# A hand-loaded activation set with logarithm and exponential in a two-block kernel

## The chip, the cores and the metric

The kernel runs on one core of one Trainium2 chip (trn2). The metric is the device time of one launch in microseconds. Five engines run side by side, each through its own list of instructions: TensorE (PE), VectorE (DVE), ScalarE (ACT), GpSimd (POOL) and SyncE (SP, which here only starts DMAs). They meet at semaphores. ScalarE evaluates its functions from tables; a set of functions is active at a time, and an instruction of its own, ACT_TABLE_LOAD, makes another set active.

## What is computed

Two transformer-like blocks, one after the other, on 512 tokens of width 1024, with 256 context tokens in the first, all in float32. Shortened from the reference:

```python
def rms(x, g):                                   # used ten times over tokens
    return x * rsqrt(mean(x * x, -1) + 1e-6) * g
# block 1
x = x + .5 * m[2] * swiglu(modulate(rms(x, g1), m[0], m[1]), w_in, w_out)      # and the same for the context
seg = modulate(rms(x, g2), m[3], m[4]) @ mix_w_in + b                          # context too
hm = mlstm(q, k, v, i, log_sigmoid(f))           # 8 heads, chunkwise, both directions
logf = log(lb + (1 - lb) * sigmoid(f)); k = (1 - lb) * sigmoid(-f)             # HGRN gates, 8 heads
o = (q * exp(b)) @ S + (q_t exp(b_t - b_s) k_s) v_s                            # b = cumsum(logf)
hh = head_rms(o) * silu(g)
x = x + m[5] * (sigmoid(gm) * (hm @ pm) + sigmoid(gh) * (hh @ ph)) @ w_out
x = rms(x + .5 * m[8] * swiglu(...), g_final)
# block 2
z = modulate(rms(x, n1), ...) @ w_in_2
attn = g0 * softmax(compressed) @ v + g1 * softmax(selected) @ v + g2 * softmax(window) @ v    # 8 heads of 64
ssm = glu(gelu(Re(C scan(a, B u)) + d * u))      # a = exp(lr*step) * (cos, sin)(li*step)
x = x + gt1 * concat(rms(attn), rms(ssm)) @ w_o
x = x + gt2 * (silu(a) * v) @ w_down             # (a, v) = causal conv(rms(x) @ w_up)
return rms(x, normf)
```

## The kernel before

The activations stay in SBUF, transposed: 128 rows of features by 512 tokens (256 for the context), eight such tiles for the width of 1024. Weights come in from HBM in tiles of 1 MB through four slots. In the feed-forwards each weight and activation is split into a rounded part and a rest (ScalarE writes `wh`, VectorE the rest `wl`), and TensorE runs three matmuls for one product; all matmuls are called through the helper at L300.

The stages follow one another: start (modulation rows, norms of x and context), feed-forward 1 (to about 680 us), the mixer's norms (to 714), the HGRN heads (to 1366), the mLSTM (to 1679), the merge (to 1988), feed-forward 2 (to 2381), the final norm of block 1 and the first of block 2, its projections (to 2564), the attention loop (to 2869), the gated output of the state-space branch, w2o (to 2952), feed-forward 3 and the last norm.

Nothing is scheduled by a planner. Each engine's order is written out by hand in a Python function per stage and engine (`act_...`, `dve_...`, `pool_...`, `pe_...`), and a wait stands where it is called: everything behind it on that engine waits too. For the HGRN heads and for the attention loop a list of items (`HG`, `B2`) is walked by all engines in the same order.

Where the change works:

- `act_stat` (L594 to L602) is ScalarE's part of a token norm: Square of each feature tile into two buffers, TensorE sums them through a matrix of ones (`pe_stat`, one matmul of two passes per tile, into a bank `ps`), then Ln (with scale 1/width and bias eps) and Exp with scale -0.5, which make the inverse root. It is called ten times; VectorE's and ScalarE's scaling waits for its Exp. In `act_ffn2` and `act_ffn3` the split of the first weight tile (L737) stands ahead of it.
- `act_hgrn` (L1135 to L1193): an item "fill" ends (at part 9) with Sigmoids of the gates and their Ln (L1160); "prep" is an Exp of a factor that GpSimd has subtracted (L1166); "state" holds further Exps; "out" is the head's output norm, Square (L1188), then Ln (L1191) and Exp (L1193). The item "out" of head h stands among the items of head h + 1, that of head 7 at the end.
- `act_mlstm` (L1401 to L1423): Exp and Ln(1 + .) of the forget gate (L1410, L1412), then Exps.
- `act_merge`: Ln and Exp of 32 columns of head norms (L1773, L1775).
- `act_att` (L2251 to L2330): in the loop over `B2`, item "exps" is the softmax's Exp of step n (L2278), "turned" the Copy of the transposed probabilities to SBUF (L2287, L2291) for TensorE's product with the values, "normed" the norm over 512 columns of a block of 128 tokens (Square L2299, Ln L2301, Exp L2303, Copy with scale L2305), "sin" the two Sin of a state-space step (L2328, L2330), in every second step. The compressed scores' Exp is L2261.

The kernel before names no set. When it is built, an ACT_TABLE_LOAD is put ahead of each activation whose function is not in the set that is active there: the first set in a fixed list that has the function. Ln and Exp get two different sets in this way. Such a load is put between the waits and the activation or ahead of them: an activation can carry a wait itself, and then the load ahead of it does not wait. In after.py the same placement still serves whatever the loads by hand leave open.

Of the kernel before, what the change touches and what calls it, by code (L numbers as in the profile page):

```python
# [317 lines left out]
def program(nc, dr, out_dram):  # L318
    ctx = ExitStack()
    with ctx:  # L320
        build(nc, dr, out_dram, ctx)


def build(nc, dr, out_dram, ctx):
# [33 lines left out]
    def rows(ap, k):  # L358
        return ap.rearrange("p (k t) -> p k t", k=k)
# [16 lines left out]
    def vec(n):  # L376
        o, c = VOFF[n]
        return VECS[:, o:o + c]
# [210 lines left out]
    def pool_start(e, w):  # L589
        ap, there = weight(("m8", 0, 1792))  # L590
        w.wait_ge(*there)
        e.tensor_copy(M8[:, :], ap).then_inc(*m8P.of("m8"))

    def act_stat(e, w, name, src, T, n_k, width, sq, rs, bank):  # L594
        for k in range(n_k):
            if k >= 2:
                w.wait_ge(*statP.at(name, k - 2))
            e.activation(sq[k % 2][:, 0:T], src[:, k, :], ACT.Square).then_inc(*statA.of(name, k))
        w.wait_ge(*statP.at(name, n_k - 1))
        e.activation(rs[:, 0:T], bank[:, 0:T], ACT.Ln, scale=1.0 / width, bias=eps).then_inc(*statA.of(name, "ln"))  # L600
        w.wait_ge(*statA.at(name, "ln"))
        e.activation(rs[:, 0:T], rs[:, 0:T], ACT.Exp, scale=-0.5).then_inc(*statA.of(name, "exp"))  # L602
# [527 lines left out]
    def act_hgrn(e, w):  # L1130
        for item, *a in HG:
            if item == "fill":
# [26 lines left out]
                for j in range(2):  # L1159
                    e.activation(z[f"b{j}"], z[f"b{j}"], ACT.Ln, scale=olb[:, j, h:h + 1],  # L1160
                                 bias=lb[:, j, h:h + 1]).then_inc(*fA.of(h, "ln", j))
            elif item == "prep":
                h, i = a
                r = RB[(14 * h + i) % 4]
                w.wait_ge(*rG.at(h, i, "k"))
                e.activation(r, r, ACT.Exp).then_inc(*rA.of(h, i))  # L1166
            elif item == "state":
                h, j, s = a
                d, b = DD[j], HD[h % 2][f"b{j}"]
                if s == 0:  # L1170
                    w.wait_ge(*sG.at(h, j, "c"))
                    e.activation(KS, KS, ACT.Exp).then_inc(*stA.of(h, j, "s"))
                    if h:
                        w.wait_ge(*oP.at(h - 1, "o"))
                    e.activation(d["qi"], b[:, 0:512], ACT.Exp).then_inc(*stA.of(h, j, "qi"))
                    e.activation(d["dc"], rows(b[:, 0:512], 4)[:, :, 127 if j == 0 else 0],
                                 ACT.Exp).then_inc(*stA.of(h, j, "dc"))
                elif s == 1:
                    w.wait_ge(*stP.at(h, j, "t1"))
                    e.activation(d["kn"][:, 0:512], banks("t1", h, j), ACT.Copy).then_inc(*stA.of(h, j, "k1"))  # L1180
                    w.wait_ge(*stP.at(h, j, "t2"))
                    e.activation(d["kn"][:, 512:768], banks("t2", h, j)[:, 0:256], ACT.Copy).then_inc(*stA.of(h, j, "k2"))
            elif item == "out":
                h, s = a
                if s == 0:
                    w.wait_ge(*oP.at(h, "o"))
                    w.wait_ge(*(fV.at(h + 1, "q") if h < 7 else oV.at(6, "u")))
                    e.activation(SB[0], banks("o", h), ACT.Square).then_inc(*oA.of(h, "sq"))  # L1188
                else:
                    w.wait_ge(*oP.at(h, "m"))  # L1190
                    e.activation(SB[0], banks("m", h), ACT.Ln, scale=1.0 / 128, bias=eps).then_inc(*oA.of(h, "ln"))  # L1191
                    w.wait_ge(*oA.at(h, "ln"))
                    e.activation(SB[0], SB[0], ACT.Exp, scale=-0.5).then_inc(*oA.of(h, "exp"))  # L1193
# [209 lines left out]
    def act_mlstm(e, w):  # L1403
        w.wait_ge(*endH[0].at(*endH[1:]))
        for k in range(1, KT, 2):
            src, dst = xp[:, k, :].rearrange("p (c r) -> p r c", r=8), xm[:, k, :].rearrange("p (r c) -> p r c", c=64)
            e.activation(dst, src, ACT.Copy).then_inc(*pmA.of("m", k))
        w.wait_ge(*pmV.at("m", KT - 2))
        w.wait_ge(*gtV.at("abs"))
        e.activation(LFs, LFs, ACT.Exp).then_inc(*gtA.of("exp"))  # L1410
        w.wait_ge(*gtA.at("exp"))
        e.activation(LFs, LFs, ACT.Ln, bias=1.0).then_inc(*gtA.of("ln"))  # L1412
        for j in range(2):
            R = slice(32 * j, 32 * j + 32)
            w.wait_ge(*gtV.at("neg", j))
            e.activation(gr[R, 512:768], gr[R, 512:768], ACT.Exp, bias=nmc[R]).then_inc(*gtA.of("wc", j))
            w.wait_ge(*gtV.at("M", j))
            e.activation(wi[R, :], Mr[R, :], ACT.Exp, scale=-1.0, bias=mC[R]).then_inc(*gtA.of("wi", j))
            w.wait_ge(*gtV.at("gu", j))
            e.activation(gu[R, :], gu[R, :], ACT.Exp, scale=-1.0).then_inc(*gtA.of("gu", j))  # L1420
        for i in range(4):
            w.wait_ge(*mlP.at("k", i))
            e.activation(kt[:, i, :], banks("k", i), ACT.Identity, bias=vec("mb_k")[:, i:i + 1]).then_inc(*mlA.of("k", i))  # L1423
# [828 lines left out]
    def act_att(e, w):  # L2252
        w.wait_ge(*cpV.at("vc"))
        w.wait_ge(*cgV.at("all"))
        w.wait_ge(*c2L.at("c2"))
        for item, n, *more in B2:
            if item == "comp":
                s = more[0]
# [52 lines left out]
            elif item == "tables":  # L2311
                i = n
                c, s = SC2[i % 2]
                if i >= 2:
                    w.wait_ge(*s5V.at(i - 2, "im"))
                    w.wait_ge(*s5G.at(i - 2, "im"))
                e.activation(s, iot, ACT.Copy, scale=c16["ph"][:, i:i + 1]).then_inc(*s5A.of(i, "sn"))
                e.activation(c, iot, ACT.Identity, scale=c16["ph"][:, i:i + 1], bias=quarter).then_inc(*s5A.of(i, "cs"))
                b = banks("bt", i)
                w.wait_ge(*s5P.at(i, "t"))  # L2320
                if i >= 2:
                    w.wait_ge(*s5P.at(i - 2, "I"))
                e.activation(BT[i % 2][0], b[:, 0:128], ACT.Copy).then_inc(*s5A.of(i, "q1"))
                e.activation(BT[i % 2][1], b[:, 128:256], ACT.Copy).then_inc(*s5A.of(i, "q2"))
            elif item == "sin":
                c, s = SC2[n % 2]
                w.wait_ge(*s5G.at(n, "cs"))
                e.activation(c, c, ACT.Sin, scale=TWO_PI).then_inc(*s5A.of(n, "cos"))  # L2328
                w.wait_ge(*s5V.at(n, "sn"))
                e.activation(s, s, ACT.Sin, scale=TWO_PI).then_inc(*s5A.of(n, "sin"))  # L2330

    def pool_att(e, w):
        for item, n, *more in B2:
# [462 lines left out]
```

## Time and profile before

| | us |
|---|---|
| three timed runs | 3377.4, 3379.3, 3381.4 (median 3379.3) |
| the profiled execution, its own time | 3383.4 |
| its span, first to last instruction | 3381.4 |
| TensorE busy in it | 3057.6 (90%) |
| VectorE | 1485.7 (44%) |
| ScalarE | 1036.6 (31%) |
| GpSimd | 527.7 (16%) |
| mean granted TensorE clock | 0.932 of 2.4 GHz |

A row of a timeline reads: start, duration, engine, line, operation, written tile <- read tiles, shapes, count; in brackets the idle time of that engine ahead of it and what ended it. Rows that follow one another closely are merged, with their count and whole duration. A helper's line (L300) stands for all its callers, so the tiles tell which call it is. A row of the waits reads: who waited for whom, microseconds in total, times, the longest. The windows give, for each stretch, the busy time and count of each engine, then PEclk, the granted TensorE clock (1.00 is 2.4 GHz, 0.50 is 1.2 GHz, between them a mixture), then the share of the DMA engines and GB/s. The busy shares are averages over stages that have different bounds; what ScalarE's time is worth shows only where another engine waits for it.

### The profile page before, as it was taken

To read this page: it belongs to the slowest core of one execution; us is meant where nothing else is said; L and a number is where in the kernel's file an instruction comes from. 1 tells how busy PE (TensorE), PEld (TensorE's weight loads), DVE (VectorE), ACT (ScalarE), POOL (GpSimd) and SP (SyncE) were. 2 spreads that over 40 slices of the span, in tenths; PEclk is the share of its full clock that TensorE was granted. 3 is DMA by queue.
4 is the path that set the end of the run, shared out by engine and by line. 5 is a ranking of instruction groups with operands and counts; after the bars stand their busy time and mean duration, and the time that the engine had idled before them with its cause. 6 is when DMAs were issued, how large, how long until landed. Compare 5 with 4: busy or idle time off the path is not lost.

```text
span 3381.4 us, 32985 instructions
## 1 busy us (share of the span) xinstructions
PE 3057.6 (90%) x13464; PEld 2269.8 (67%) x13464; DVE 1485.7 (44%) x2473; ACT 1036.6 (31%) x1605; POOL 527.7 (16%) x498
## 2 busy tenths in 40 slices
PE   7999999979888987898899989999798788999997
PEld 3888888846666665665566567877356555377785
DVE  0866555215444556305731142332214887143443
ACT  3311111143333344103421132222313556152432
POOL 0000010004322233000001101000002655010210
PEclk9999999989999998998899999999995787999999
DMA  7344444021101000210021222222121000222220
GB/s 276 122 165 181 152 160 153 15 81 38 38 26 38 25 13 1 91 62 13 13 75 75 83 86 93 95 97 83 38 75 50 7 7 13 88 86 87 81 95 36
DMA packets 36726, 254.82 MB, mean 75 GB/s; under 512 B 4064, under 2 KB 4192, under 8 KB 10080
## 3 DMA queue, kind: packets, MB, share of 16 engines
q1 hardware_dynamic: 36576, 252.73, 20.6%
q8 instruction: 106, 1.74, 0.2%
q14 instruction: 44, 0.36, 0.0%
HBM read 250.61 MB, written 2.10 MB: 75 GB/s over the span
## 4 chain that ended last, share of the span: by engine, by line
PE 79%; DVE 10%; ACT 6%; POOL 2%; issue 2%; DMA 0%; DVEq 0%; SPq 0%; POOLq 0%; another core or an unknown queue 0%; ACTq 0%
PE ps L300 78%; DVE xm L1238 1%; DVE at L1245 1%; POOL tb L2351 1%; DVE xs L767 1%; DVE t L762 0%; DVE wb L2486 0%; DVE hd L1212 0%; POOL kb L2339 0%; DVE hd L1214 0%; ACT hd L1152 0%; ACT L602 0%; ACT hd L1150 0%; ACT L600 0%; POOL cs L2341 0%
## 5 line engine op out<-in xcount | busy, mean ns | idle before, releaser
L300 PE MATMUL ps<-xs,wh 128*128 128x512 f32 (+1 forms) x3328 | 955.2, 372 | 30.5 <-DVE xs L767 20.6
L300 PEld LDWEIGHTS ps<-xs,wh 128*128 128x128 f32 x3328 | 603.8, 190 | 147.7 <-issue 24.4
L300 PE MATMUL ps<-xs,wl 128*128 128x512 f32 (+1 forms) x1664 | 614.5, 369 | 0.0
L300 PE MATMUL ps<-h,wh 128*128 128x512 f32 (+1 forms) x1408 | 402.9, 373 | 34.9 <-POOL h L906 34.9
L743 DVE TENSOR_TENSOR wl<-w,wh 128x2048 fp32r<-128x2048 f32 (+3 forms) x122 | 264.6, 2168 | 229.0 <-ACT wh L737 229.0
L737 ACT ACTIVATE wh<-w 128x2048 fp32r<-128x2048 f32 (+3 forms) x122 | 221.0, 1811 | 440.0 <-PE ps L300 361.2
L300 PEld LDWEIGHTS ps<-xs,wl 128*128 128x128 f32 x1664 | 316.3, 190 | 53.6
L300 PEld LDWEIGHTS ps<-h,wh 128*128 128x128 f32 x1408 | 260.0, 194 | 81.9 <-issue 37.6
L300 PE MATMUL ps<-h,wl 128*128 128x512 f32 (+1 forms) x704 | 261.3, 371 | 0.0
L300 PE MATMUL ps<-xp,w 128*128 128x512 f32 x512 | 231.4, 597 | 10.7 <-ACT xp L1005 10.7
L906 POOL TENSOR_TENSOR h<-t,h 128x512 fp32r<-128x512 f32 x66 | 73.0, 1111 | 944.3 <-ACT h L839 944.3
L300 PE MATMUL ps<-xm,w 128*128 128x512 f32 (+1 forms) x464 | 176.1, 549 | 21.7 <-DMA w<-in_wgate 11.2
L698 DVE SCALAR_TENSOR_TENSOR sq<-w,small,sq 128x256 f32<-128x256 f32 x392 | 180.8, 483 | 10.0
L300 PEld LDWEIGHTS ps<-xm 128*128 128x128 f32 x896 | 124.1, 205 | 79.8 <-issue 74.7
L300 PE MATMUL ps<-xm 128*128 128x128 f32 x896 | 127.2, 290 | 49.2 <-DVE xm L1238 49.2
L300 PEld LDWEIGHTS ps<-xp,w 128*128 128x128 f32 x512 | 94.1, 192 | 109.4 <-issue 98.2
L300 PEld LDWEIGHTS ps<-xm,w 128*128 128x128 f32 x464 | 90.8, 227 | 104.6 <-issue 102.9
L884 DVE SCALAR_TENSOR_TENSOR x<-ps,small,x 128x512 f32<-128x512 f32 x80 | 60.0, 750 | 220.8 <-PE ps L300 220.8
L300 PEld LDWEIGHTS ps<-h,wl 128*128 128x128 f32 x704 | 136.6, 194 | 22.6
L839 ACT ACTIVATE h<-t 128x512 fp32r<-128x512 f32 x66 | 37.0, 560 | 372.1 <-DVE t L862 372.1
L1113 POOL TENSOR_TENSOR xm<-hd 128x256 f32<-128x256 f32 x112 | 84.9, 758 | 382.0 <-DVE hd L1212 294.4
L862 DVE TENSOR_TENSOR t<-t,ps 128x512 f32<-128x512 f32 x66 | 39.5, 599 | 197.3 <-PE ps L300 191.5
(388 smaller groups left out, 4133.3 us busy)
## 6 DMA issues: line engine op xcount, KB each, us to landing
w<-in_ada SPq DMA_DIRECT2D x60, 1024.0 KB, 4.8
w<-in_f1i SPq DMA_DIRECT2D x22, 1024.0 KB, 5.7
w<-in_f2i SPq DMA_DIRECT2D x22, 1024.0 KB, 4.8
w<-in_f3i SPq DMA_DIRECT2D x22, 1024.0 KB, 4.8
w<-in_whf SPq DMA_DIRECT2D x8, 1024.0 KB, 4.8
w<-in_whqg SPq DMA_DIRECT2D x8, 1024.0 KB, 4.7
w<-in_wgg SPq DMA_DIRECT2D x8, 1024.0 KB, 6.8
w<-in_wpp SPq DMA_DIRECT2D x8, 1024.0 KB, 4.8
```

The lines of the kernel that those rows point to most:

```text
L300: return e.matmul(out, l, r, start=st, stop=sp)
L698: e.scalar_tensor_tensor(out=a, in0=wv[:, k, :], scalar=v[:, k:k + 1], in1=a, op0=ALU.mult, op1=ALU.add).then_inc(*mvV.of(n, c, k))
L737: e.activation(hi[:, 0:key[2]], ap, ACT.Copy).then_inc(*hiA.of(key))
L743: e.tensor_tensor(lo[:, 0:key[2]], ap, hi[:, 0:key[2]].bitcast(F32), ALU.subtract).then_inc(*loV.of(key))
L767: e.scalar_tensor_tensor(out=lo[:, k, :], in0=ybuf[(i - 1) % 3][:, 0:T], scalar=shift[:, k:k + 1], in1=hi[:, k, :].bitcast(F32), op0=ALU.a ...
L839: e.activation(hh_[:, q, o:o + T], s[:, 0:T], ACT.Copy).then_inc(*hidA.of(F.name, j, x))
L862: e.tensor_tensor(s, s, banks(F.name, j, 1, x)[:, 0:T], ALU.mult).then_inc(*gateV.of(F.name, j, x))
L884: e.scalar_tensor_tensor(out=dst[:, m, :], in0=banks(F.name, n, "dn", m, x)[:, 0:T], scalar=g[:, m:m + 1], in1=dst[:, m, :], op0=ALU.mult, ...
L906: e.tensor_tensor(hl_[:, q, o:o + T], s, hh_[:, q, o:o + T].bitcast(F32), ALU.subtract).then_inc(*hidP.of(F.name, j, x))
L1113: e.tensor_tensor(rv[:, :, qh, :], b4[:, :, qh, :], mid, ALU.subtract).then_inc(*rG.of(h, i, "q"))
L1238: e.tensor_tensor(Ev[:, :, kh, :], rv[:, :, kh, :], factor_views(z[f"k{j}"][:, 0:512], hf)[:, :, kh, :], ALU.mult).then_inc(*eV.of(h, i, "k"))
L1245: e.copy_predicated(rows(AT[j][h % 2], 4), m8v[:, j, n, :].unsqueeze(1).to_broadcast([128, 4, 128]), rows(banks("prod", h, i), 4)).then_in ...
```

## The change

A function `logs` loads the set `natural_log_exp_and_others`, which holds Ln and Exp. It is called at the start of every `act_stat`, after the two gate Ln of each HGRN head, after the Ln of the mLSTM gates (ahead of which the set `natural_log` is loaded by hand), at the start of the attention loop behind its three waits, and after the second Sin of each state-space step. While that set is active no further load is placed for Ln, Exp, Square, Copy or Identity.

```diff
--- before.py
+++ after.py
@@ -591,7 +591,12 @@
         w.wait_ge(*there)
         e.tensor_copy(M8[:, :], ap).then_inc(*m8P.of("m8"))
 
+    def logs(e):
+
+        e.preload_act_table_set("natural_log_exp_and_others")
+
     def act_stat(e, w, name, src, T, n_k, width, sq, rs, bank):
+        logs(e)
         for k in range(n_k):
             if k >= 2:
                 w.wait_ge(*statP.at(name, k - 2))
@@ -1159,6 +1164,7 @@
                 for j in range(2):
                     e.activation(z[f"b{j}"], z[f"b{j}"], ACT.Ln, scale=olb[:, j, h:h + 1],
                                  bias=lb[:, j, h:h + 1]).then_inc(*fA.of(h, "ln", j))
+                logs(e)
             elif item == "prep":
                 h, i = a
                 r = RB[(14 * h + i) % 4]
@@ -1408,8 +1414,10 @@
         w.wait_ge(*pmV.at("m", KT - 2))
         w.wait_ge(*gtV.at("abs"))
         e.activation(LFs, LFs, ACT.Exp).then_inc(*gtA.of("exp"))
+        e.preload_act_table_set("natural_log")
         w.wait_ge(*gtA.at("exp"))
         e.activation(LFs, LFs, ACT.Ln, bias=1.0).then_inc(*gtA.of("ln"))
+        logs(e)
         for j in range(2):
             R = slice(32 * j, 32 * j + 32)
             w.wait_ge(*gtV.at("neg", j))
@@ -2253,6 +2261,7 @@
         w.wait_ge(*cpV.at("vc"))
         w.wait_ge(*cgV.at("all"))
         w.wait_ge(*c2L.at("c2"))
+        logs(e)
         for item, n, *more in B2:
             if item == "comp":
                 s = more[0]
@@ -2328,6 +2337,7 @@
                 e.activation(c, c, ACT.Sin, scale=TWO_PI).then_inc(*s5A.of(n, "cos"))
                 w.wait_ge(*s5V.at(n, "sn"))
                 e.activation(s, s, ACT.Sin, scale=TWO_PI).then_inc(*s5A.of(n, "sin"))
+                logs(e)
 
     def pool_att(e, w):
         for item, n, *more in B2:
```

The program has 114 table loads before and 79 after: 36 by hand through `logs`, one by hand of `natural_log`, 42 placed by the build. All else stays in its order.

ScalarE at the mixer's norm of x (`act_stat` "mx", then `act_shift`), before:

```order
L598 ACTIVATE t<-x 128x512 [waits ffn_acc]
L598 ACTIVATE t<-x 128x512
L598 ACTIVATE t<-x 128x512 [waits stat_pe] x6
L600 ACT_TABLE_LOAD
L600 ACTIVATE t<-ps,small 128x512 [waits stat_pe]
L602 ACT_TABLE_LOAD
L602 ACTIVATE t<-t 128x512 [waits stat_act]
```

and in the change:

```order
L596 ACT_TABLE_LOAD [waits ffn_acc]
L603 ACTIVATE t<-x 128x512 x2
L603 ACTIVATE t<-x 128x512 [waits stat_pe] x6
L605 ACTIVATE t<-ps,small 128x512 [waits stat_pe]
L607 ACTIVATE t<-t 128x512 [waits stat_act]
```

One load instead of two, and it carries the wait for the feed-forward (`ffn_acc`) that the first Square carried.

ScalarE around the output norm of HGRN head 5, in the items of head 6 (`hd`, `xm` gates and factors, `s` the norm's buffer), before:

```order
L1160 ACT_TABLE_LOAD
L1160 ACTIVATE hd<-hd,small 128x768 [waits hg_fill_act]
L1160 ACTIVATE hd<-hd,small 128x768
L1166 ACT_TABLE_LOAD
L1166 ACTIVATE xm<-xm 128x512 [waits hg_log_pool] x4
L1188 ACTIVATE s<-ps 128x512 [waits hg_fill_dve,hg_out_pe]
L1166 ACTIVATE xm<-xm 128x512 [waits hg_log_pool]
L1191 ACT_TABLE_LOAD
L1191 ACTIVATE s<-ps,small 128x512 [waits hg_out_pe]
L1193 ACT_TABLE_LOAD
L1193 ACTIVATE s<-s 128x512 [waits hg_out_act]
```

and in the change:

```order
L1165 ACT_TABLE_LOAD
L1165 ACTIVATE hd<-hd,small 128x768 [waits hg_fill_act]
L1165 ACTIVATE hd<-hd,small 128x768
L596 ACT_TABLE_LOAD
L1172 ACTIVATE xm<-xm 128x512 [waits hg_log_pool] x4
L1194 ACTIVATE s<-ps 128x512 [waits hg_fill_dve,hg_out_pe]
L1172 ACTIVATE xm<-xm 128x512 [waits hg_log_pool]
L1197 ACTIVATE s<-ps,small 128x512 [waits hg_out_pe]
L1199 ACTIVATE s<-s 128x512 [waits hg_out_act]
```

The load behind the gate Ln stands where it stood, with another set; the two of the output norm are gone.

ScalarE in the attention loop, at the first Sin (`cs` its tables, `pt` the transposed probabilities), before:

```order
L2328 ACT_TABLE_LOAD
L2328 ACTIVATE cs<-cs 128x512 [waits s5_pool]
L2330 ACTIVATE cs<-cs 128x512 [waits s5_dve]
L2287 ACTIVATE pt<-ps 128x256 [waits att_turn_pe]
L2278 ACT_TABLE_LOAD
L2278 ACTIVATE xm,small<-ps,small 128x128 [waits att_max]
```

and in the change:

```order
L2337 ACT_TABLE_LOAD
L2337 ACTIVATE cs<-cs 128x512 [waits s5_pool]
L2339 ACTIVATE cs<-cs 128x512 [waits s5_dve]
L596 ACT_TABLE_LOAD
L2296 ACTIVATE pt<-ps 128x256 [waits att_turn_pe]
L2287 ACTIVATE xm,small<-ps,small 128x128 [waits att_max]
```

The load for Exp has moved ahead of the Copy.

## Rows read from the trace of the kernel before

**Rows 1.** The page: busy time by engine; the chain that ended last, by engine.

```profile
PE 3057.6 (90%) x13464; PEld 2269.8 (67%) x13464; DVE 1485.7 (44%) x2473; ACT 1036.6 (31%) x1605; POOL 527.7 (16%) x498
...
PE 79%; DVE 10%; ACT 6%; POOL 2%; issue 2%; DMA 0%; DVEq 0%; SPq 0%; POOLq 0%; another core or an unknown queue 0%; ACTq 0%
```

**Rows 2.** Timeline, the mixer's norm of x.

```profile
680.00 7.49 PE L300 MATMUL ps<-t,cst 128*128 128x512 f32 x16 [1.33 <-ACT t L598]
...
686.33 1.28 ACT L600 ACT_TABLE_LOAD   x1
687.63 0.69 ACT L600 ACTIVATE t<-ps,small 128x512 f32<-128x512 f32 x1
688.33 1.28 ACT L602 ACT_TABLE_LOAD   x1
```

**Rows 3.** Windows: sums of the norm at 2383 and of that at 2891.

```profile
2383.00:2386.00 3.00, 3.00 (x7) 1.18 (x8) 0.00 (x0) 1.66 (x4) 0.00 (x0) 1.00 0.00 0
...
2891.30:2894.00 2.70, 2.63 (x4) 1.23 (x5) 0.00 (x0) 1.17 (x3) 0.00 (x0) 0.61 0.72 303
```

**Rows 4.** Timeline, TensorE's sums in three norms, with the idle time ahead.

```profile
1990.71 9.18 PE L300 MATMUL ps<-t,cst 128*128 128x512 f32 x16 [3.40 <-ACT t L598]
...
2382.94 7.49 PE L300 MATMUL ps<-t,cst 128*128 128x512 f32 x16 [1.60 <-ACT t L598]
...
2891.37 5.40 PE L300 MATMUL ps<-tb,cst 128*128 128x512 f32 x8 [2.17 <-ACT tb L598]
```

**Rows 5.** Timeline, start: first Squares, and TensorE's modulation rows.

```profile
11.44 1.15 ACT L598 ACTIVATE sq<-x 128x512 f32<-128x512 f32 x2 [4.67 <-DMA x<-in_x]
...
32.18 41.60 PE L300 MATMUL ps<-w,small 128*2 128x256 f32 x192
```

**Rows 6.** Timeline, the mixer's norm of the context: sums and Ln.

```profile
696.98 6.15 PE L300 MATMUL ps<-t,cst 128*128 128x256 f32 x16 [9.49 <-ACT t L598]
...
703.69 0.47 ACT L600 ACTIVATE t<-ps,small 128x256 f32<-128x256 f32 x1
```

**Rows 7.** Waits of TensorE in the HGRN stage, 790 to 1372 us.

```profile
PE ps L1346 <- DVE xc L1260: 5.6, 1, 5.6
```

**Rows 8.** Timeline, output norms of heads 6 and 7: mean, then Ln.

```profile
1324.57 1.08 PE L300 MATMUL ps<-s,cst 128*128 128x512 f32 x2
...
1326.30 0.69 ACT L1191 ACTIVATE s<-ps,small 128x512 f32<-128x512 f32 x1
...
1360.20 1.13 PE L300 MATMUL ps<-s,cst 128*128 128x512 f32 x2 [0.69 <-ACT s L1188]
...
1361.46 0.69 ACT L1191 ACTIVATE s<-ps,small 128x512 f32<-128x512 f32 x1
```

**Rows 9.** Timeline, the merge's head norms: VectorE's reductions and Ln.

```profile
1688.40 4.68 DVE L1812 TENSOR_REDUCE small<-xmc 128x8 f32<-128x1024 f32 x4
...
1693.14 0.32 ACT L1773 ACTIVATE small<-small 128x32 f32<-128x32 f32 x1
```

**Rows 10.** Timeline, ScalarE's entry into the attention loop.

```profile
2571.83 1.28 ACT L2261 ACT_TABLE_LOAD   x1 [7.54 <-DVE xm L2380]
```

**Rows 11.** Timeline, a Copy behind Sin and the product that reads it.

```profile
2589.21 0.36 ACT L2287 ACTIVATE pt<-ps 128x256 f32<-128x256 f32 x1
...
2592.48 0.66 PE L300 MATMUL ps<-vn,pt 128*128 128x64 f32 x4
```

**Rows 12.** Waits of TensorE in the attention loop, 2570 to 2905 us.

```profile
PE ps L2581 <- DVE bb L2454: 37.6, 11, 7.7
PE ps L2574 <- ACT rp L2305: 14.9, 3, 10.8
```

**Rows 13.** Timeline, the end of the attention loop: TensorE and GpSimd.

```profile
2867.88 1.12 PE L2574 MATMUL ps<-cst,rp 128*128 128x128 f32 x4 [10.84 <-ACT rp L2305]
2868.79 4.92 PE L300 MATMUL ps<-wb,w 128*128 128x512 f32 x8
...
2868.96 1.65 POOL L2358 TENSOR_TENSOR wb<-wb,tb 128x512 f32<-128x512 f32 x1 [1.23 <-DVE wb L2488]
```

## The prediction

> **What bounds the kernel now.** I read the profile in this order: busy time by engine, the chain that ended last, then, for every place that the change touches, the timeline of all engines around it, the waits of TensorE and the granted clock. Busy time and chain say that TensorE is the bound: 90% of the span busy, 79% of the chain, while ScalarE is busy 31% and holds 6% of the chain [rows 1]. So a table load taken from ScalarE is worth something only where TensorE (or, in the attention loop, VectorE) is waiting for the ScalarE instruction behind it. By the order of instructions the program has 114 table loads before and 79 after. 35 loads of 1.28 us are 44.9 us of ScalarE; the question is how much of that lies on the path.
>
> **A norm.** Of a norm (the eight Squares, Ln, Exp) the reader is to see two things [rows 2]. The load ahead of Ln starts at 686.33, right behind the last Square, while TensorE still sums that Square until 687.49 (680.00 + 7.49); Ln starts at 687.63. So this load is covered but for 0.14 us. The load ahead of Exp (688.33) has no cover: Ln has just ended. The change removes both and puts one load ahead of the first Square. There ScalarE has just been released by a wait, and a load put in by hand stands behind that wait, where one put in by the builder stands ahead of it (the order rows show which instruction carries the wait). Nothing covers it, because the Squares, and TensorE's sums of them, are what everybody waits for. One load with its gap is 1.30 us. A norm is then: + 1.30 (new) - 1.30 (Exp's) - 0.14 (Ln's open rest) = -0.1.
>
> **The clock in a norm.** What precedes the sums decides how long they take. Where TensorE has been idle 1.60 us, the 16 matmuls take 7.49 us and the granted clock stays 1.00 (2.4 GHz); after 2.17 us idle it is 0.61 over the first stretch, that is mostly the 1.2 GHz level, and after 3.40 us idle the 16 matmuls take 9.18 us [rows 3, 4]. Three norms start warm today: the one at 680 (idle 1.33, [rows 2]), the one at 2383 (idle 1.60) and the last one of the kernel (7.49 us as well). The new load lengthens these idles to 2.6, 2.9 and 2.9 us, beyond the 2.17 us after which the clock is seen to fall. I take the fall in all three: 3 x (9.18 - 7.49) = +5.1. Its bounds are 0 and 5.1. The other norms start cold anyway.
>
> **All norms.** The first pair, on x and on the context, is special. The Squares on x start when their DMA has landed, and the load now stands behind that wait. The context's Squares follow with a second load of a set that is already active. TensorE's 192 matmuls for the modulation rows follow without a gap until 73.8 [rows 5], so what is late at their start is late at their end; the values of Ln and Exp are wanted only after them. From the start: + 1.3 - 0.1 - 1.3 + 1.3 = +1.2. The norm of the context after the first feed-forward sums half as many columns, so its Ln load is covered less: the sums end at 703.13, Ln starts at 703.69 [rows 6]; + 1.3 - 1.3 - 0.5 = -0.5. Six more norms (at 680, 1990, 2383, 2399, 2955, 3362) give -0.1 each, -0.7 with rounding. The norm of the four tiles behind the gate of the state-space branch gives 0. Together 0.0. Loading a set that is already active was not seen; I take the full 1.28 us, for a load is a copy whatever was there, and keep 0 as its other end for four of these loads.
>
> **HGRN heads.** Per head the change removes the two loads of the output norm (Ln, Exp), and moves the load of the first factor's Exp to stand right behind the two gate Ln, where its neighbours in ScalarE's order are the same: the move is worth nothing. In heads 0 to 5 the output norm falls in a stretch in which TensorE works through the next head's projections: in the whole stage TensorE waits once for the factor chain behind an output norm (L1346, 5.6 us) [rows 7], and that is at head 6, with no projections left. There TensorE has the mean ready at 1325.65 and Ln starts at 1326.30; without loads Ln starts 0.6 earlier and Exp a further 1.3. At head 7 it is 1361.33 against 1361.46, so 0.1 + 1.3 [rows 8]. Behind it hang the output, the slot for the gate weights and their DMA, all of which move along. HGRN: -1.9 - 1.4 = -3.3.
>
> **mLSTM and merge.** In the mLSTM gates a load stays before Ln and one moves; TensorE is busy all through, 0. In the merge, Ln starts at 1693.14 because VectorE reduces until 1693.08 (1688.40 + 4.68): its load was covered. Exp's load was not, and TensorE waits for what hangs on it [rows 9]: -1.3.
>
> **Attention loop.** Its first load waits with ScalarE for VectorE and sits open on the chain (2571.83) [rows 10]; by hand it is placed ahead of that wait: -1.3. In the 16 steps with Sin, the load for Exp moves ahead of the Copy between them. Exp comes when it did. The Copy comes 1.28 us later, and TensorE's value product reads it; here the Copy ends at 2589.57 and the product starts at 2592.48 [rows 11], the smallest gap I found in these steps, so it stays covered: 0. The four norms of 512 columns lose two loads each. TensorE waits three times for them, 14.9 us in all and 10.8 the longest, so 4.1 in the other two; but in the same loop it waits 37.6 us for VectorE's tables [rows 12], which shows VectorE to be the next bound there. Bounds 0 and -4.1; I take -0.4, near the VectorE end. The last of the four ends the loop: TensorE starts at 2867.88 for it and would start 2.6 earlier. But the last state sums need GpSimd's xi, done at 2870.61 (2868.96 + 1.65). Today TensorE's eight matmuls run from 2868.79 to 2873.71 [rows 13], the first four at about 0.85 us each; begun at 2866.2, four end at 2869.6, the other four wait until 2870.65 and end at about 2872.4: -1.3, with 0 and -2.6 as bounds.
>
> **The sum.** Norms 0.0, HGRN -3.3, merge -1.3, entry of the loop -1.3, its norms -0.4, its end -1.3: -7.6. With the clock of three norms, +5.1: -2.5. The profiled execution took 3383.4 us, its span 3381.4, and the median of the runs is 3379.3; I apply the difference to the median: 3376.8. All of this is near 0.1%, and 0.2% (6.8 us) is about what a measurement of this kernel can tell from no change.
>
> A rule of the skill speaks for more. The Trainium skill, "ScalarE: Activation LUTs", section "Rules for kernel authors", says that a kernel needing Exp and Ln should use the set that holds both, for one load and not two. The trace agrees on the price of a load but not on its worth: in a norm the first of the two is under TensorE's sums and the new one is open. The same page, "What ACT_TABLE_LOAD costs", adds a drain to each switch, 2.66 us in all; the trace has Ln start 0.02 us behind its load's end. With 2.66 for 1.30, -7.6 would be some -14 and the time about 3370.
>
> **Rivals.** (1) The clock stays at 2.4 GHz in all three norms, their idles being still under the 3.40 us that surely lost it: -7.6, 3371.7. For it: only one row lies between 1.60 and 3.40. Chance 0.17. (2) Every load counts, as a rule that counts loads would have it: 35 x 1.28, 3334.4. Against it speaks the whole of [rows 1]. Chance 0.02. (3) Loading an active set is nearly free: four loads less (context, context after the feed-forward, and the norms at 2399 and 2955): -2.5 - 5.1 = -7.6, also 3371.7. Chance 0.05. (4) Slower: the Copies are on the path after all. It decides where less than 1.28 us lies between a Copy and the product that reads it; if all 16 steps give up 1.28, + 20.5 - 2.5 = +18.0, 3397.3; five of them suffice to be slower than before. The gap of 2.9 us speaks against it. Chance 0.05. (5) The removed waits only let TensorE run into VectorE or a DMA sooner, so that HGRN and merge give back half, with the falls: -0.2, 3379.1. Chance 0.11. My forecast: 0.60.
>
> **Numbers.** 3376.8 is the forecast; a fall in one or two norms only gives 3375.1 or 3373.4, inside it. The range 3370.5 to 3381.5 takes in (1), (3) and (5), the full 4.1 of the attention norms on one side and none of the uncertain gains on the other, and leaves out (2), (4) and the tails. Faster by over 0.2% needs (1), (3) or (2), in part, 0.2; slower is (4) and a tail, 0.06; within 0.2% 0.74.
>
> **What would show it.** ScalarE's busy time falls by about 45 us and the span by 3. In a norm, a load of 1.28 us ahead of the Squares with nothing beside it, and Ln and Exp without. A granted clock near 0.5 in the sums at 681, 2384 and 3364, their 16 matmuls at over 9 us. The rows product at start beginning 1.2 later; TensorE's wait at L1346 (now L1352) shorter by 1.9 and its wait ahead of the merge by 1.3. If the three norms keep 7.49 us, the clock step is wrong; if Copies show TensorE waiting in the loop, (4) is right.

## The result: 0.2% slower in one comparison, even in the second, and the profile after

Thirteen executions each, in one comparison: 3386.3 us (median, 3379.6 to 3390.7) against 3378.6 for the kernel before; ratio 1.0021, interval 1.0013 to 1.0030. A second comparison of the same two kernels, below, gave 1.0001 (0.9990 to 1.0012). Over all 27 executions of the changed kernel and all 75 of the kernel before on record, the means are 3384.4 and 3380.8: +3.5 us, 0.10%. These come from several comparisons, whose medians for the kernel before alone lie between 3378.6 and 3382.5, so the pooled figure is rough. The prediction, 3376.8 with a range up to 3381.5, is wrong: the gain that it forecast came in neither comparison, and the first one lies outside the range.

The page of the changed kernel, to be held against [rows 1]: span, busy time by engine, the chain by engine.

```profile
span 3387.5 us, 32949 instructions
...
PE 3070.5 (91%) x13464; PEld 2278.5 (67%) x13464; DVE 1487.9 (44%) x2473; ACT 994.3 (29%) x1570; POOL 528.1 (16%) x498
...
PE 79%; DVE 11%; ACT 5%; POOL 2%; issue 2%; DMA 0%; DVEq 0%; SPq 0%; POOLq 0%; another core or an unknown queue 0%; ACTq 0%
```

ScalarE lost 42.3 us of work, near the 44.9 us of 35 loads. TensorE became 12.9 us *busier* with the same 13,464 matmuls. In these traces matmuls of one shape take longer where the granted clock is lower ([rows 3, 4]: sums at 1.00 and at 0.61), and the mean clock fell from 0.932 to 0.929: the first hint.

The mixer's norm, timeline; it answers to [rows 2]:

```profile
679.08 1.28 ACT L596 ACT_TABLE_LOAD   x1 [20.11 <-DVE xc L889]
680.38 1.15 ACT L603 ACTIVATE t<-x 128x512 f32<-128x512 f32 x2
681.15 7.49 PE L300 MATMUL ps<-t,cst 128*128 128x512 f32 x16 [2.61 <-ACT t L603]
...
688.68 0.69 ACT L605 ACTIVATE t<-ps,small 128x512 f32<-128x512 f32 x1 [1.22 <-PE ps L300]
689.40 0.63 ACT L607 ACTIVATE t<-t 128x512 f32<-128x512 f32 x1
```

The load stands open ahead of the Squares; Ln and Exp follow without one. From the start of the sums to the start of Exp it is 8.25 us, before 9.62: 1.37 less, for 1.28 more of idle time ahead of the sums. The norm gives back what the load took, and 0.1. The sums keep 7.49 us although TensorE was idle for 2.61 ahead of them. All 36 loads of the joint set take the same time, also the four that find it active:

```profile
L596 ACT ACT_TABLE_LOAD  x36: 1283/1283/1283, 11.7 to 3365.2; - x36
```

Two more norms, at 1993 and at the end of the kernel; and the eight sums behind the gate of the state-space branch. The first and the third answer to [rows 4]:

```profile
1992.67 9.81 PE L300 MATMUL ps<-t,cst 128*128 128x512 f32 x16 [4.82 <-ACT t L603]
...
3367.26 10.30 PE L300 MATMUL ps<-t,cst 128*128 128x512 f32 x16 [2.88 <-ACT t L603]
...
2896.91 3.83 PE L300 MATMUL ps<-tb,cst 128*128 128x512 f32 x8 [3.45 <-ACT tb L603]
```

The last norm in the kernel before:

```profile
3362.61 7.49 PE L300 MATMUL ps<-t,cst 128*128 128x512 f32 x16 [1.60 <-ACT t L598]
```

The last norm lost the clock after 2.88 us idle (0.70 over its 16 sums); the one at 2385, after the same 2.88, did not (7.49). And behind the gate TensorE was idle 3.45 us, longer than the 2.17 of [rows 4], and its sums took 3.83, at clock 1.00, in place of 5.40. How long it was idle does not decide this alone.

**Where the time went.** Every kernel here has the same 13,464 matmuls in the same order, so the start of the n-th one can be compared between two traces. The columns give how much later the changed kernel leaves each stage than it entered it, for two pairs: the first two traces (spans 3387.5 and 3381.4), and two further executions of the same kernels described below (3378.2 and 3375.9). The figures in brackets are the falls of the clock that the prediction put on three norms.

| stage | predicted | first pair | second pair |
|---|---|---|---|
| start, to the modulation rows | +1.2 | -0.1 | +0.7 |
| feed-forward 1 | 0 | 0.0 | +1.6 |
| norms at 680 and 697 | -0.6 (+1.7) | +0.1 | +0.2 |
| HGRN heads, to the gate weights | -3.3 | -2.1 | -3.3 |
| mLSTM | 0 | +1.6 | -0.3 |
| merge | -1.3 | -0.3 | -0.7 |
| its projections, to 1990 | 0 | +1.4 | 0.0 |
| norm at 1990 | -0.1 | +0.7 | +1.3 |
| feed-forward 2 | 0 | -0.3 | -0.1 |
| norms at 2383 and 2399, first projections | -0.2 (+1.7) | +1.7 | +2.0 |
| further projections | 0 | +1.7 | +1.6 |
| entry of the attention loop | -1.3 | -1.4 | -1.4 |
| the loop, its norms, its end | -1.7 | +1.3 | +1.5 |
| gated output, w2o | 0 | -0.7 | -0.7 |
| norm at 2955, feed-forward 3 | -0.1 | -0.2 | -0.1 |
| last norm, to the end | -0.1 (+1.7) | +2.7 | 0.0 |
| sum | -2.5, with +5.1 for the clock | +6.1 | +2.3 |

In the first pair eight stages lose time, and two of them (3.1 us) contain nothing that the change touches; in the second pair it is two of seven (3.2 us). The +1.6 of the mLSTM, where one load has moved and one is another set's, is not in the second pair.

One of these losses is no scatter. From the first matmul behind the norm at 2399 to the last projection ahead of the attention loop, the same 462 matmuls, first in the kernel before and then in the changed one (window, its length, busy time and count of each engine, granted clock, DMA share, GB/s):

```profile
2413.50:2564.40 150.90, 139.09 (x462) 84.14 (x462) 32.69 (x86) 21.93 (x49) 8.88 (x7) 0.90 0.17 64
```

```profile
2414.90:2568.70 153.80, 141.99 (x462) 86.26 (x463) 32.68 (x86) 21.91 (x49) 8.87 (x7) 0.88 0.18 63
```

The 2.9 us are TensorE's busy time: 1.3 of them arise within 6 us of the first of these matmuls, 1.6 from 2530 to 2537, behind a pause of 3.2 us that is the same in both kernels. Both traces of the kernel before take 150.9, all four of the changed kernel 153.8 to 153.9, and the kernels of experiments 1, 2 (the norms' loads alone) and 5 below 153.7 to 153.9; the three that leave the norms as they were take 150.9 to 151.1, and those of experiments 4 and 7 149.2. So this loss goes with where the loads of the norms stand, in every trace. How they cause it is not shown: the kernel of experiment 1 pays it too, though TensorE idles no longer ahead of its sums than before.

### The profile page after: what moved, and what is told of

Its sections match the earlier page's. It is cut to its first block, busy times and chain, and to the rows that moved or that the text cites. A ratio compares the mean times of both kernels' runs of the same rounds, so it can differ in the third digit from the quotient of the medians.

```text
span 3387.5 us, 32949 instructions
## 1 busy us (share of the span) xinstructions
PE 3070.5 (91%) x13464; PEld 2278.5 (67%) x13464; DVE 1487.9 (44%) x2473; ACT 994.3 (29%) x1570; POOL 528.1 (16%) x498
## 4 chain that ended last, share of the span: by engine, by line
PE 79%; DVE 11%; ACT 5%; POOL 2%; issue 2%; DMA 0%; DVEq 0%; SPq 0%; POOLq 0%; another core or an unknown queue 0%; ACTq 0%
PE ps L300 79%; DVE xm L1244 1%; POOL tb L2361 1%; DVE at L1251 1%; DVE wb L2496 1%; DVE xs L772 1%; DVE t L767 0%; POOL kb L2349 0%; DVE hd L1218 0%; ACT L596 0%; DVE wb L2492 0%; DVE hd L1220 0%; ACT hd L1157 0%; POOL cs L2351 0%; ACT hd L1155 0%
```

## Experiments

**1. The load behind the Squares.** The same load and count, placed later:

```diff
     def act_stat(e, w, name, src, T, n_k, width, sq, rs, bank):
-        logs(e)
         for k in range(n_k):
...
+        logs(e)
         w.wait_ge(*statP.at(name, n_k - 1))
```

> The changed kernel with one thing moved: in each of the eleven norms the load of the joint set stands behind the last Square, ahead of the wait for TensorE's sums, and no longer ahead of the first Square. 79 loads as in the changed kernel. Theory A (the load ahead of the Squares is open, 1.30 us in each norm, and lengthens the idle time of TensorE that precedes the sums, so that the clock falls in some): the last norm's 16 sums are back at 7.49 us (10.30 in the changed kernel), each norm ends about 1.3 earlier than in the changed kernel, and the whole is 10 to 16 us faster than the changed kernel, that is 3 to 9 us faster than the kernel before (ratio 0.9974 to 0.9991). Theory B (the norms are nearly even, and the attention loop and its Copies make the kernel slower): 0 to 4 us faster than the changed kernel, ratio 1.001 to 1.002. Theory C (the joint set itself makes its instructions slower): as the changed kernel, 1.002.

Measured: 3369.9 us, ratio 0.9966 (0.9954 to 0.9978), 12.6 below the median of the kernel before. Against the changed kernel in the same comparison it is 12 below the mean and 9.7 below the median, where theory A gave 10 to 16. (There are ten norms; "eleven" was a miscount.) Theory A holds in size for the step between the two kernels; the gain over the kernel before is more than the 3 to 9 us that it gave, since the changed kernel was no slower than that one here. B and C fall. The last norm's sums are back at 7.50 us. The norm at 1990 in this kernel:

```profile
1979.39 9.06 PE L300 MATMUL ps<-t,cst 128*128 128x512 f32 x16 [3.40 <-ACT t L602]
...
1986.64 0.63 ACT L602 ACTIVATE t<-x 128x512 f32<-128x512 f32 x1 [0.23 <-PE ps L300]
1987.29 1.28 ACT L596 ACT_TABLE_LOAD   x1
1988.59 0.69 ACT L605 ACTIVATE t<-ps,small 128x512 f32<-128x512 f32 x1
1989.31 0.63 ACT L607 ACTIVATE t<-t 128x512 f32<-128x512 f32 x1
```

The load lies where the load ahead of Ln lay in [rows 2], beside TensorE's last sum, and serves Exp as well.

**2. The norms alone, and all but the norms.** The first adds to the kernel before only

```diff
     def act_stat(e, w, name, src, T, n_k, width, sq, rs, bank):
+        logs(e)
```

and the second takes only this line from the changed kernel.

> The kernel before with the new load ahead of the first Square of each norm, and nothing else of the change: 104 loads. Theory A (the norms hold the loss): slower than before by 6 to 10 us, ratio 1.0018 to 1.0030. Theory B (the attention loop holds it): ratio 0.9995 to 1.0005. By the stages of the two traces so far, the norms at 1990, 2383 and 3362 us end 0.7, 1.2 and 2.7 us later.

> The changed kernel without the load in the norms (they keep the loads ahead of Ln and of Exp as before); HGRN heads, merge and attention loop as changed: 89 loads. Theory A: 1 to 5 us faster than the kernel before, ratio 0.9985 to 0.9997. Theory B: 4 to 7 us slower, ratio 1.0012 to 1.0021.

Measured, norms alone: 3391.2 us (3380.6 to 3397.0), ratio 1.0022 (1.0010 to 1.0034). All but the norms: 3380.6, ratio 0.9996 (0.9988 to 1.0005). So what loses lies in the norms, and what the rest brings is not the 7.6 us predicted for it, but 1.9, within what the comparison can tell from nothing.

**3. The changed kernel again, three times, and the kernel before again.** No edit.

> The changed kernel once more, for the scatter between profiled executions: which differences of a stage come again. Every theory: ratio 1.0013 to 1.0030. Theory A: the sums of the last norm take 9 us or more again, and the norms at 680 and 2383 keep 7.49. If the differences inside the attention loop and of the granted clock ahead of it (2536 us) come with another sign, they are scatter and no effect of the change.

> The changed kernel, one more execution, to compare one of its shorter executions (3377 to 3381) with its longer ones (3387 to 3392) stage by stage. Theory G: they differ only where the granted clock differs: in the norms (the last one 7.49 against 10.30), in the feed-forwards and in the attention loop, with waits for other engines alike. Rival: one stage holds the 10 us, with a wait of its own.

> As the look before it: the changed kernel, one more execution. Theory G: sums of the norms at 680 and 2383 can take 7.49 or over 9 us from one execution to the next. Rival: they are the same in each.

> The kernel before, one more execution. Theory G: its stages differ from those of its first trace only by the granted clock, up to 2 us in mLSTM (where three kernels lost 1.4 us and four did not) and up to 4 us in the attention loop; its norms at 680, 2383 and 3362 take 7.49 us again, since they follow after 1.33 and 1.60 us without work.

Measured: the repeat gave ratio 1.0001, outside what every theory had said, with eight executions from 3376.7 to 3380.0 and four from 3388.8 to 3392.3. Two single executions gave 3391.8 and 3380.3, so one of each sort has a trace; the kernel before gave 3377.8. The page's busy time, first of the longer and then of the shorter one:

```profile
span 3389.8 us, 32949 instructions
...
PE 3071.2 (91%) x13464; PEld 2280.4 (67%) x13464; DVE 1487.0 (44%) x2473; ACT 994.1 (29%) x1570; POOL 528.1 (16%) x498
```

```profile
span 3378.2 us, 32949 instructions
...
PE 3060.1 (91%) x13464; PEld 2271.2 (67%) x13464; DVE 1486.1 (44%) x2473; ACT 993.6 (29%) x1570; POOL 528.4 (16%) x498
```

11.1 of the 11.6 us are TensorE's busy time. No stage holds them: by the start of the same matmuls the longer one loses 2.6 at the start, 1.6 in feed-forward 1, 1.5 in HGRN, 1.8 in mLSTM, 1.5 at 1938, 2.9 in feed-forward 2, and nothing from there to the end, the attention loop among it. At 1938 nothing stands but a matrix product; a window there in the longer and then in the shorter one (busy time and count of each engine, granted clock, DMA share, GB/s):

```profile
1938.00:1948.00 10.00, 7.78 (x19) 4.26 (x19) 6.04 (x9) 2.43 (x2) 1.66 (x1) 0.83 0.50 195
```

```profile
1929.00:1939.00 10.00, 7.78 (x24) 4.03 (x23) 5.10 (x7) 2.44 (x2) 1.66 (x1) 1.00 0.42 153
```

TensorE is busy 7.78 of 10 us in both; in one the clock dips, in the other it doesn't, and then 24 matmuls run in the time of 19. Theory G holds in that the clock makes the difference. Its places are wrong: the attention loop differs by nothing, and the sums at 680 and 2383 took 7.49 us in all four traces of the changed kernel, those of the last norm in three of the four. The kernel before shows the same: its second trace is 5.5 us shorter than its first, 4.9 of it TensorE's busy time (3052.7 for 3057.6), with 1.7 at the start and 3.1 in feed-forward 1 and nothing in the mLSTM or the attention loop, where up to 2 and up to 4 had been expected; its three warm norms took 7.49 again. The Trainium skill, "TensorE: Matmul & The Clock Gate", Part 1, says that the same kernel meets the clock gate differently from one run to the next. The traces agree, with 11.1 us of TensorE's busy time between two executions of this kernel.

Of the 27 executions of the changed kernel 11 took over 3387 us, of the 75 of the kernel before 3; of the 12 with the norms' loads alone 7 did; of the 33 of the three kernels that leave the norms as they were (all but the norms, and experiment 6), none took over 3384.4. Within the second comparison alone it is 4 of 12, 3 of 30, 7 of 12 and 0 of 11.

**4. Early: the load ahead of the wait.** At the six places where the norm finds another set, for instance

```diff
         act_ffn(e, w, F2)
+        logs(e)
         w.wait_ge(*end2[0].at(*end2[1:]))
         act_stat(e, w, "fin", xv, TL, KT, D, f2_tmp, f2_tmp[2], banks("fin"))
```

and none in the four others, which find it active: 75 loads, four fewer than in experiment 1.

> The changed kernel with the norm's load written ahead of the wait that precedes the norm (so that it falls into idle time of ScalarE), and left out in the four norms that find the joint set already active: 75 loads. Theory A (a norm costs what is open in it, and a load behind a wait is open): TensorE's idle time ahead of the sums is back at 1.33 and 1.60 us (2.6 and 2.9 in the changed kernel), Ln and Exp have no load ahead; each norm is as short as in the kernel with the late load or 0.1 to 0.6 shorter, the time 3366 to 3371, ratio 0.9955 to 0.9978. Rival D (the late load gained by something else than the load's place, such as a draw of the clock): 3375 or more, ratio 0.998 or more.

Measured: 3367.1 us, ratio 0.9956 (0.9944 to 0.9969). It is the best kernel of the study, 14.2 us below the median of the kernel before in its comparison. The last norm:

```profile
3330.68 1.28 ACT L596 ACT_TABLE_LOAD   x1
3348.78 1.15 ACT L602 ACTIVATE t<-x 128x512 f32<-128x512 f32 x2 [16.81 <-DVE x L889]
```

```profile
3349.55 7.49 PE L300 MATMUL ps<-t,cst 128*128 128x512 f32 x16 [1.60 <-ACT t L602]
...
3357.08 0.69 ACT L604 ACTIVATE t<-ps,small 128x512 f32<-128x512 f32 x1 [1.22 <-PE ps L300]
3357.80 0.63 ACT L606 ACTIVATE t<-t 128x512 f32<-128x512 f32 x1
```

The load takes 1.28 us of 18 in which ScalarE has nothing to do, and TensorE's idle time is back at 1.60. Rival D falls: two kernels with different places of the load, both covered, agree within 3 us.

**5. Double: two loads ahead of the Squares.**

```diff
     def act_stat(e, w, name, src, T, n_k, width, sq, rs, bank):
+        e.preload_act_table_set("natural_log")
         logs(e)
```

> The changed kernel with two loads ahead of the Squares of each norm (first the set of the logarithm, then the joint one): 89 loads. Theory A: each of the ten norms ends 1.30 us later than in the changed kernel, 10 to 13 us in all, and where TensorE is then idle for more than 4 us ahead of the sums, these take 9 us or more in all norms, also at 680, 2383 and 3362: 12 to 20 us slower than the changed kernel, ratio to the kernel before 1.0035 to 1.0065. Rival (the loads are covered and only the draw of the clock differs): ratio 1.000 to 1.0025.

Measured: 3403.2 us, ratio 1.0063 (1.0050 to 1.0076), at the upper end of theory A, 19 us above the mean of all executions of the changed kernel. The last norm, which answers to the two above:

```profile
3375.91 1.28 ACT L599 ACT_TABLE_LOAD   x1 [18.10 <-DVE x L890]
3377.20 1.28 ACT L596 ACT_TABLE_LOAD   x1
...
3379.27 9.06 PE L300 MATMUL ps<-t,cst 128*128 128x512 f32 x16 [4.17 <-ACT t L604]
```

Now all three warm norms lose the clock: 9.88 us after 3.90 idle at 685, 9.06 after 4.17 at 2393 and here. So up to 2.88 us of idle time the clock nearly always held in these three places, and at 3.90 and 4.17 us it did not. Elsewhere the same does not hold, as the gate branch shows. In one table, the time from TensorE's last matmul ahead of a norm to its first behind it (the last norm has none behind; its 16 sums stand there):

| norm | before | changed | norms alone | late | early | double |
|---|---|---|---|---|---|---|
| 680 and 697 | 35.2 | 35.3 | 35.3 | 32.7 | 32.4 | 40.0 |
| 1990 | 17.8 | 18.5 | 18.7 | 16.4 | 16.3 | 19.7 |
| 2383 and 2399 | 32.2 | 32.6 | 32.7 | 30.1 | 29.8 | 36.6 |
| gate branch | 7.4 | 7.1 | 10.0 | 5.8 | 8.0 | 10.5 |
| 2955 | 17.7 | 17.7 | 18.3 | 14.9 | 17.4 | 20.2 |
| last, sums | 7.5 | 10.3 | 7.5 | 7.5 | 7.5 | 9.1 |

One profiled execution each, so a unit or two is the clock's; but the first three rows show the order plainly. Covered, the joint set is worth 1.0 to 1.5 us for each norm of the first three rows (two of them hold two norms); open, nothing or less.

**6. The parts outside the norms, one at a time.** To the kernel before are added, in the first kernel, the loads in HGRN and mLSTM (the merge follows from the set that is then active); in the second, those of the attention loop:

```diff
                                  bias=lb[:, j, h:h + 1]).then_inc(*fA.of(h, "ln", j))
+                logs(e)
...
+        e.preload_act_table_set("natural_log")
         w.wait_ge(*gtA.at("exp"))
         e.activation(LFs, LFs, ACT.Ln, bias=1.0).then_inc(*gtA.of("ln"))
+        logs(e)
```

```diff
         w.wait_ge(*c2L.at("c2"))
+        logs(e)
         for item, n, *more in B2:
...
                 e.activation(s, s, ACT.Sin, scale=TWO_PI).then_inc(*s5A.of(n, "sin"))
+                logs(e)
```

> The kernel before with the change in the HGRN heads, the mLSTM gates and the merge alone. The prediction gave -3.3 and -1.3: 4.6 us faster, ratio 0.9986. By the stages of the traces of the changed kernel, -2.1 in the heads, 0 to +1.4 in mLSTM, -0.3 in the merge: 0.6 to 2.4 faster, ratio 0.9990 to 1.0000.

> The kernel before with the change in the attention loop alone. The prediction gave -3.0 us, ratio 0.9991. By the stages of the traces of the changed kernel the entry gives -1.4 and the rest of the loop takes 1 to 3 back: ratio 0.9998 to 1.0005. If the Copies of the Sin steps were on the path, over 1.002.

Measured: HGRN to merge 3378.2 us, ratio 0.9992 (0.9983 to 1.0001); attention 3381.7, ratio 1.0002 (0.9993 to 1.0011). The interval of the first holds both its values. The second is on the side of the stages: no gain where 3 us were predicted. TensorE's waits in the loop of the second say where they went, against [rows 12] (2568 to 2903 us, the same columns):

```profile
PE ps L2587 <- DVE bb L2460: 46.4, 11, 7.7
PE ps L2580 <- ACT rp L2310: 7.8, 1, 7.8
```

The wait for the loop's norms fell by 7.1 us, the wait for VectorE's tables rose by 8.8. The wait for the Copy that a Sin load delays stays at 0.8 us, once, as before. That VectorE took the gain back is read from these waits and not isolated, for the loop's length also moves with the clock: without any edit in it, it took 306.4 us in both traces of the kernel before, 302.2 with the norms' loads alone and 302.8 in the first kernel here, with TensorE busy 248.4, 239.2 and 246.0 (the same 939 matmuls, behind the entry).

**7. The loop as before, behind the early norms.** From kernel 4 the load behind the two Sin is taken out:

```diff
                 e.activation(s, s, ACT.Sin, scale=TWO_PI).then_inc(*s5A.of(n, "sin"))
-                logs(e)
```

> The kernel with the early norm loads, without the load behind each pair of Sin: in the attention loop only the load at the entry is written by hand, the rest is placed as in the kernel before (82 loads). Theory E (the joint set in the loop gains nothing, since TensorE's wait for the loop's norms goes over to VectorE, and the two executions with and without it differ by -2 to +4 us through the clock): within 3 us of the kernel with the early loads, 3364 to 3368, ratio 0.9950 to 0.9965; TensorE waits some 15 us for the loop's norms and some 37 us for VectorE's tables, in place of 8 and 46. Theory F (the loads behind Sin delay the loop by 2 us or more): 3362 to 3365, ratio 0.9940 to 0.9952. By the prediction's terms, which gave the norms and the end of the loop 1.7 us: 3368 to 3370.

Measured: 3368.2 us, ratio 0.9965 (0.9952 to 0.9979), at the upper edge of theory E and at the lower one of the prediction's terms; one microsecond can't be told here. The waits are 12.9 for the norms and 43.3 for the tables, not the 15 and 37 expected: together 56.2 with the old loop and 54.6 (7.8 and 46.8) with the new one. The loop's loads are worth nothing that these runs can measure.

## Why the prediction failed, step by step

Two steps failed. The clock term was put on three norms (+5.1) and at nothing everywhere else: the norms' clock held in eleven of twelve cases, and the clock was lost in stages that the prediction had at 0. And the attention loop's norms and end, at -1.7, measured +1.3 and +1.5. The steps in order:

**The norm's arithmetic** held at 680 (-0.1, measured -0.1, idle time and sums to Exp together). It failed at 1990: there TensorE has been idle 4.82 us in place of 3.40 and more of its sums run at 1.2 GHz, 9.81 us for 9.18. A norm that starts cold can get worse too; I had taken it to be without risk. In all four traces of the changed kernel these sums took 9.78 to 10.41. At the start the rows product begins 1.4 us later on the mean of five traces with the change (32.15) than of five with the old start (30.72); predicted +1.2, near it, though the first pair alone (32.04 and 32.18) hides it and the two groups overlap (31.18 to 33.75, and 30.13 to 32.18).

**The clock step** had the right sign and the wrong place; that its size, 5.1, is of the order of what the clock took elsewhere is chance. I took one row (2.17 us idle, clock 0.61) as the point at which the clock falls, and put +1.7 on each of three norms. In twelve such norms (three in each of four traces) it fell once, and in the three of the kernel with the norms' loads alone not at all. The loss came elsewhere, in stages that the sum has at 0: 2.9 us in the projections ahead of the attention loop in every trace of the changed kernel, and in the longer executions also in feed-forward 1, the mLSTM, the products to 1990 or feed-forward 2. With the norms' loads alone the kernel is 8.7 us slower by the medians, where the table of norms and the start account for about 6, 2.6 of it at the gate branch; the rest is not placed. Its one trace is of a shorter execution (3385.4), in which the projections take 2.9 more than before and the loop 4.2 less. I had written that a trace can be compared with a trace and the difference put on the median; with executions that spread over 15.6 us (3376.7 to 3392.3 in the second comparison), and where 11.1 of the 11.6 us between two traced ones are TensorE's busy time, that holds for no effect of 3 us.

**HGRN** was right. TensorE's longest wait at L1352 is 3.7 us, 5.6 in [rows 7] (a second, short one there makes 5.0 in all); head 7 is shorter by 1.4. The waits of the changed kernel, then head 7 before and changed:

```profile
PE ps L1352 <- DVE xc L1266: 5.0, 2, 3.7
```

```profile
1364.12 0.75 DVE L1279 SCALAR_TENSOR_TENSOR s<-ps,vec,s 128x512 f32<-128x512 f32 x1 [8.57 <-ACT s L1193]
```

```profile
1360.58 0.69 ACT L1197 ACTIVATE s<-ps,small 128x512 f32<-128x512 f32 x1 [1.22 <-PE ps L300]
1361.30 0.63 ACT L1199 ACTIVATE s<-s 128x512 f32<-128x512 f32 x1
1361.96 0.75 DVE L1285 SCALAR_TENSOR_TENSOR s<-ps,vec,s 128x512 f32<-128x512 f32 x1 [7.19 <-ACT s L1199]
```

It answers to [rows 8]; VectorE's idle time fell from 8.57 to 7.19 us. The stage is 3.3 us shorter in the second pair, 2.1 in the first, whose clock dipped before head 7.

**The merge** was right where it was argued. VectorE waits 0.65 us for Exp, 1.96 before, 1.3 less. Before, then changed:

```profile
1695.03 4.63 DVE L1818 TENSOR_TENSOR hn<-hn,small 128x1024 f32<-128x1024 f32 x4 [1.96 <-ACT small L1775]
```

```profile
1692.71 0.32 ACT L1781 ACTIVATE small<-small 128x32 f32<-128x32 f32 x1 [1.29 <-DVE small L1820]
1693.06 0.23 ACT L1783 ACTIVATE small<-small 128x32 f32<-128x32 f32 x1
...
1693.32 4.63 DVE L1826 TENSOR_TENSOR hn<-hn,small 128x1024 f32<-128x1024 f32 x4 [0.65 <-ACT small L1783]
```

Of this the stage keeps 0.3 in the first pair and 0.7 in the second.

**The entry of the loop** was right, -1.3 against -1.4 in each of the traces of kernels with this load.

**The loop's norms and its end** were wrong by 3 us. I had named VectorE as the next bound for the norms and still took a gain at the end, reckoning with GpSimd's `xi` at a fixed time. It moved, since it hangs on the same VectorE. The end of the loop, against [rows 13]:

```profile
2868.77 1.11 PE L2584 MATMUL ps<-cst,rp 128*128 128x128 f32 x4 [7.76 <-ACT rp L2314]
2869.68 3.62 PE L300 MATMUL ps<-wb,w 128*128 128x512 f32 x4
...
2872.41 1.65 POOL L2368 TENSOR_TENSOR wb<-wb,tb 128x512 f32<-128x512 f32 x1 [1.23 <-DVE wb L2498]
2874.21 3.75 PE L300 MATMUL ps<-wb,w 128*128 128x512 f32 x4 [0.91 <-POOL wb L2368]
```

TensorE comes to the norm only 0.9 us later than before although the kernel is 3 us late there, so the norm did give its 2 to 3 us. But `xi` ends 3.45 us later than before, the last four matmuls wait for it and take 3.75 us (granted clock 0.50, the 1.2 GHz level): I had them end 1.75 behind it.

**Rivals.** (1), the clock holds in all three norms, came true in three of the four traces, and its time, 3371.7, did not come: the clock was lost elsewhere. (3) is excluded: an active set is loaded in full 1.28 us. (2) is excluded. (4), Copies on the path, is excluded by the wait of 0.8 us that did not grow and by experiment 7, where the kernel without these loads is no faster; its price also had a slip, for two steps of 1.28 us, not five, would have eaten the 2.5 us. (5), gains given back, came true in the attention loop and the merge, not in HGRN. What the prediction lacked was a rival in which the clock costs time in stages that the change doesn't touch, and a price for it.

**Left open:** what makes an execution one of the longer ones. With the load ahead of the Squares they are more frequent (11 of 27 and 7 of 12, against 3 of 75 and none of 33), and of the 11.6 us between two of them 11.1 are TensorE's busy time; why an open 1.3 us in a norm brings a lower clock 100 us away, no run here shows.

## What to carry to other kernels

Fewer table loads are worth nothing by their count: a joint set gained here where its one load lay in time that ScalarE had anyway, ahead of a wait or beside another engine's last work, and gained nothing or lost where it was written behind a wait, even if it replaced two. The changed kernel gave 1.0021 and 1.0001, with the norms' loads ahead of the Squares; with them in covered places it gave 0.9966 and 0.9956. Where executions of one kernel differ by more than the effect that is sought, take several traces of both kernels, and compare the start of the same instruction stage by stage, before a cause is given to a difference.

## What the hardware showed that was not expected

- The granted clock of one and the same kernel differs from execution to execution at places far from any idle time of note: 11.1 us of TensorE's busy time between two executions on the same chip. Another loss comes the same in every trace of the changed kernel: 2.9 us in the projections ahead of the attention loop, which no edit touches.
- An idle time of 2.61 to 2.88 us ahead of the sums of the three warm norms cost the clock in one of fifteen cases, 3.90 to 4.17 in three of three. At the gate branch the idle time ahead decides nothing: after 2.17 us the eight sums took 5.40 us in three traces and 3.83 in three others, after 3.45 us 3.83 in all four of the changed kernel and 6.67 with the norms' loads alone.
- A load of the set that is already active takes 1.283 us like any other.
